# Output projection of the second block's mixer: the gate goes into the weights of columns 512 to 1023, on GpSimd

## The chip, the core and the metric

The kernel runs on one core of a Trainium2 chip, as one launch. Its time is device microseconds of that core. Several runs are made; the median counts. One further execution is recorded by the hardware profiler, and all rows of a trace in this document come from such an execution. The engines are TensorE (PE, its weight loads PEld), VectorE (DVE), ScalarE (ACT), GpSimd (POOL) and SyncE (SP, which here only issues transfers). All work side by side and wait for one another through semaphores.

## The reference

Two transformer blocks of different kinds run one after the other on 256 tokens of width 1024, all in float32. The first has an mLSTM mixer, a pooling mixer, cross attention and squared-ReLU layers. The second, to which the change belongs, has one layer:

```
mod = c_act @ w_ada[l] + b_ada[l]
sh_a, sc_a, g_a, sh_f, sc_f, g_f = jnp.split(mod[:, None, :], N_MOD, axis=-1)
h = rms_norm(x, g_mix[l]) * (1.0 + sc_a) + sh_a
x = x + g_a * hybrid_mixer(h, ...)      # ends in: return merged @ w_out
h = rms_norm(x, g_ffn[l]) * (1.0 + sc_f) + sh_f
x = x + g_f * swiglu(h, w_gate[l], w_up[l], w_down[l])
...
return rms_norm(x, g_final)
```

hybrid_mixer has four heads of differential attention ("diff") and four of latent attention ("mla"), both causal. merged is 256 x 1024 and w_out 1024 x 1024. The gate g_a is one number per output column, the same for all tokens, so g_a * (merged @ w_out) equals merged @ (w_out with column c times g_a[c]).

## The kernel before, in words

Tokens lie in two tiles of 128 partitions, t = 0 and 1. Each 1 MB piece of a weight ("chunk", 128 x 2048 float32 in SBUF) is loaded by SP into one of four buffers (raw), and then split into a high part in PE's rounded format and a low rest: ACT casts raw into wh (hi_to, line 1193), DVE subtracts, wl = raw - wh (lo_to, line 1841; lo_part, line 1849, in pieces). Activations are split the same way (XH and XL, in the trace XS). PE multiplies high by high, high by low and low by high. A raw buffer is loaded anew once DVE has made wl from it.

The chunks of the output projection are named wout2 0 to 3; each holds 256 rows of w_out with all 1024 columns. They are loaded, cast and split in the order 0, 2, 1, 3, which SP, ACT, DVE and PE follow. PE's rows("wout2", ...) (lines 406, 413 and 421) sums them into four PSUM banks: YB[2t] for columns 0 to 511 of token tile t, YB[2t + 1] for columns 512 to 1023. The last two chunks are summed in one call, tile 0 ahead of tile 1.

Each engine runs one program written out by hand, in the order of its lines; nothing is scheduled later. While PE works on attention, DVE and ACT do its softmaxes between their shares of the weight splits:

- diff_e(h) on DVE (lines 2465 to 2469) scales and subtracts the two softmaxes of a diff head, in a tile U (reciprocal, TENSOR_SCALAR, then twice a TENSOR_SCALAR and a SCALAR_TENSOR_TENSOR). PE's diff_t(h) transposes that tile (line 1012).
- mla_e(h) on DVE (lines 2501 to 2503) scales the softmax of an mla head, also in U, and mla_t(h) transposes it (line 1012).
- diff_v(h): ACT sums squares, POOL makes the reciprocal root (lines 2831 and 2728, named "do"), DVE scales (2477).

Behind the last sum, DVE's gated adds the projection to the residual rows X: a product with the gate's row (line 2590) and an addition (line 2591), for each tile and each half h of the columns:

```
e.wait_ge(*pe_rows[rows, t, h])
e.wait_ge(d_gate, 32)
step(e.tensor_tensor(U[:, t, cs], YB[2 * t + h][:, :], GB[:, n, cs], ALU.mult))
e.tensor_tensor(X[:, t, cs], X[:, t, cs], U[:, t, cs], ALU.add).then_inc(cnt.add(("gated", t, h)))
```

GB (a part of AR) holds the two gates' rows on all partitions; POOL loads it at 627. step lets the engine wait for its own instruction. Then follow the mean square (rms_square, rms_mean, and rsqrt on POOL), the scaled rows U = X * r (rms_z, line 2327, or ACT's line 1537), PE's transposes of U (line 512), and the columns' scale and shift with a new split (ACT lines 1356 and 1361, DVE lines 2073, 2077 and 2082). With these blocks PE starts the first gate and up products of the feed-forward part (pair, line 474). For the last down projection, chunks ("down", 9) and ("down", 10), POOL already multiplies columns 512 to 1023 of raw with the second gate (line 2842) ahead of ACT's cast.

Of the kernel before, what the change touches and what calls it, by code (L numbers as in the profile page):

```python
# [11 lines left out]
ALU = mybir.AluOpType  # L12
# [6 lines left out]
NR = 4  # L19
# [143 lines left out]
def build_program(nc, I, out):  # L163
    ctx = ExitStack()
    with ctx:
        def sb(name, shape, dt=F32):
            return ctx.enter_context(nc.sbuf_tensor(name, shape, dt))

        def sem(name):
            return ctx.enter_context(nc.semaphore(name))  # L170
# [3 lines left out]
        def count(name):  # L174
            counts.append(Count(sem(name)))
            return counts[-1]
# [3 lines left out]
        RAW = [sb(f"raw{i}", [128, CH]) for i in range(NR)]  # L180
        WH = [sb(f"wh{i}", [128, CH], F32R) for i in range(NS)]
        WL = [sb(f"wl{i}", [128, CH], F32R) for i in range(NS)]
        X = sb("X", [128, 2, 1024])
# [22 lines left out]
        YB = [ctx.enter_context(nc.psum_tensor(f"YB{i}", [128, 512], F32)) for i in range(4)]  # L206
# [4 lines left out]
        def cols(key, n):  # L211

            if key not in sm_at:
                a = max((b for _, b in sm_at.values()), default=0)
                sm_at[key] = (a, a + n)
                assert a + n <= 416
            a, b = sm_at[key]
            return SM[:, a:b]
# [41 lines left out]
        GB = AR[:, 6144:8192].rearrange("p (n c) -> p n c", n=2)  # L260
# [43 lines left out]
        N = {c[0]: n for n, c in enumerate(chunks)}  # L304
# [4 lines left out]
        landed = lambda n: (s_raw[n % NR], 16 * sum(len(parts(i)) for i in range(n % NR, n + 1, NR)))  # L309
# [5 lines left out]
        d_idn, d_cols, d_tab, d_mem, d_crow, d_gate, d_ln10, d_gm, d_wm, d_tb, d_lam, d_out0, d_out1 = (  # L315
            sem("in_" + n) for n in "idn cols tab mem crow gate ln10 gm wm tb lam out0 out1".split())
# [8 lines left out]
        w_hi, w_lo, w_hi0, w_lo0, w_ada, w_pool, w_gated, w_lat_hi, w_lat_lo = (  # L325
            count(n) for n in "w_hi w_lo w_hi0 w_lo0 w_ada w_pool w_gated w_lat_hi w_lat_lo".split())
        pe_turn, pe_front, pe_mlstm, pe_rows, pe_xa, pe_mlp, pe_pool, pe_mix, pe_ffn = (
            count("pe_" + n) for n in "turn front mlstm rows xa mlp pool mix ffn".split())
        act_front, act_mlstm, act_y, act_ln, act_xa, act_mlp, act_pool, act_mix, act_ffn = (
            count("act_" + n) for n in "front mlstm y ln xa mlp pool mix ffn".split())  # L330
        dve_zero, dve_front, dve_mlstm, dve_y, dve_ln, dve_xa, dve_mlp, dve_mod, dve_mix, dve_ffn = (
            count("dve_" + n) for n in "zero front mlstm y ln xa mlp mod mix ffn".split())
# [842 lines left out]
        def scalar(e):  # L1175
            at, steps_ = [0], Steps(act_own)

            def hi_to(m):

                while at[0] < len(mms) and at[0] <= m:  # L1180
                    k = at[0]
                    at[0] += 1
                    n = mms[k]
                    name, _, a, b = chunks[n]
                    raw, w = RAW[n % NR], WH[k % NS]
                    e.wait_ge(*(w_gated[n] if name in (("down", 9), ("down", 10)) else landed(n)))
                    if k >= NS:
                        e.wait_ge(*ends.get(k - NS, (act_own, 1)))
                    if name[0] == "qup":
                        for o, s in qup_parts(w, raw):  # L1190
                            f = e.copy(o, s)
                    else:
                        f = e.copy(w[:, 0:a * b], raw[:, 0:a * b])  # L1193
                    f.then_inc(w_hi.add(k))
# [35 lines left out]
            m, n = M["in", 1], N["in", 1]  # L1230
# [26 lines left out]
            for j in range(4):  # L1257
# [5 lines left out]
                for t in range(2):  # L1263
                    W = bank_of.get(("vo", j, t), WB[0])
                    e.wait_ge(*pe_front["vo", j, t])
                    if j < 2:
                        f = e.copy(V1[:, t, 2 * j:2 * j + 2, 0:256], W[:, :].rearrange("p (h c) -> p h c", h=2))
                    else:
                        f = e.activation(OG[:, t, 512 * j - 1024:512 * j - 512], W[:, :], ACT.Sigmoid)
# [514 lines left out]
            r = [cols(("rms", "out", t), 6)[:, 3:4] for t in range(2)]  # L1784
# [4 lines left out]
            for h in range(2):  # L1789
                cs = slice(512 * h, 512 * h + 512)  # L1790
                e.wait_ge(*dve_ffn["g", 0, h])
                f = e.activation(U[:, 0, cs], U[:, 0, cs], ACT.Identity, scale=r[0])
# [15 lines left out]
        def vector(e):  # L1808
            at, steps_ = [0, 0], Steps(dve_own)

            def step(f):
                f.then_inc(steps_.add())
                e.wait_ge(*steps_.now())

            def lo_to(m):


                while at[0] < len(chunks) and at[1] <= m:
                    n = at[0]
                    at[0] += 1  # L1820
                    name, _, a, b = chunks[n]
                    raw = RAW[n % NR]
                    if name[0] == "ada":
                        e.wait_ge(*landed(n))
                        e.wait_ge(d_crow, 32)
                        for i in range(2):
                            w, c = raw[:, 1024 * i:1024 * i + 1024], 2 * name[1] + i
                            f = e.scalar_tensor_tensor(w, w, 1.0, CROW, ALU.mult, ALU.mult, accum_out=MS[:, c:c + 1])  # L1828
                        f.then_inc(w_ada.add(n))
                        continue  # L1830
                    if name in (("pool",), ("lat", 1), ("lat", 2)):
                        continue
                    m_ = at[1]
                    at[1] += 1
                    H, L = WH[m_ % NS], WL[m_ % NS]
                    e.wait_ge(*w_hi[m_])
                    if name[0] == "qup":
                        for (h, s), (l, _) in zip(qup_parts(H, raw), qup_parts(L, raw)):
                            f = e.tensor_tensor(l, s, h.bitcast(F32), ALU.subtract)
                    else:  # L1840
                        f = e.tensor_tensor(L[:, 0:a * b], raw[:, 0:a * b], H[:, 0:a * b].bitcast(F32), ALU.subtract)  # L1841
                    f.then_inc(w_lo.add(m_))
# [19 lines left out]
            for q in range(4):  # L1862
# [10 lines left out]
                if q == 1:  # L1873
                    e.wait_ge(*act_front["gates"])
                    for o, c in ((0, 0), (32, 4)):
                        p = e.tensor_tensor(GL[:, :, o:o + 4], GRAW[:, :, c:c + 4], GH[:, :, o:o + 4].bitcast(F32),
                                            ALU.subtract)
# [708 lines left out]
            def gated(rows, cnt, n, t, h):  # L2586
                cs = slice(512 * h, 512 * h + 512)
# [3 lines that stand above are left out]
                e.tensor_tensor(X[:, t, cs], X[:, t, cs], U[:, t, cs], ALU.add).then_inc(cnt.add(("gated", t, h)))  # L2591

            g, b = lambda k: MC[:, 32 + k:33 + k], lambda k: MC[:, 24 + k:25 + k]
            lo_to(M["gate", 0])
            gated("wout2", dve_mix, 0, 0, 0)
            gated("wout2", dve_mix, 0, 0, 1)
            rms_square("ffn", 0, 1, dve_mix["gated", 0, 1])
            rms_mean("ffn", 0, (act_ln["ms", "ffn", 0, 0], dve_ln["ms", "ffn", 0, 1]))
            lo_part(M["up", 0], 0, 512)
# [1 line left out]
            lo_part(M["up", 0], 512, 1024)  # L2601
            gated("wout2", dve_mix, 0, 1, 0)
            evac("ffn", 0, 1, g, b)
            gated("wout2", dve_mix, 0, 1, 1)
            lo_part(M["up", 0], 1024)
            rms_low("ffn", 0, 0)
            rms_mean("ffn", 1, (act_ln["ms", "ffn", 1, 1],))
# [30 lines left out]
            for t in range(2):  # L2638
                ts = slice(256 * t, 256 * t + 256)
                e.wait_ge(*act_ffn[("g", 0) if t else ("g", 0, "first")])  # L2640
                p = e.tensor_tensor(SU[0][:, ts], YB[t][:, 256:512], SG[0][:, ts], ALU.mult)
# [57 lines left out]
            w, last = cols(("rms", "out", 1), 6), X[:, 1, 768:1024]  # L2699
# [10 lines left out]
        def gpsimd(e):  # L2710
# [16 lines left out]
            def rsqrt(o, x, sem_):  # L2727
                e.tensor_tensor(o, x, MH[:, 0:o.shape[1]], ALU.pow).then_inc(sem_)
# [13 lines left out]
            for h in range(4):  # L2742
                for t in range(2):
                    w = cols(("hc", h, t), 4)
# [45 lines left out]
            n, s_in = bvec("scale", I["pool_scale"][0])  # L2790
            p = N["pool",]
# [3 lines left out]
            for k in range(2):  # L2795
                f = e.tensor_tensor(r4[:, :, k], r4[:, :, k], BV[n][:, :].rearrange("p (g c) -> p g c", g=4), ALU.mult)
# [25 lines left out]
            for t in range(2):  # L2822
                for name, n in (("kl", 256), ("ql", 384)):
                    w = cols((name, t), 2)
                    e.wait_ge(*act_mix[name, t])
                    step(e.tensor_scalar(w[:, 0:1], w[:, 0:1], 1 / n, EPS, ALU.mult, ALU.add))
                    rsqrt(w[:, 1:2], w[:, 0:1], po_mix.add((name, t)))
            for h in range(4):
                w = cols(("do", h), 4)
                e.wait_ge(*act_mix["osq", h])  # L2830
                step(e.tensor_scalar(w[:, 0:2], w[:, 0:2], 1 / 128, EPS, ALU.mult, ALU.add))
                rsqrt(w[:, 2:4], w[:, 0:2], po_mix.add(("do", h)))
            rms_stats("ffn")
            users[:] = [dve_ln["z", "ffn", 1, 1]] * 2
            bvec("final", I["g_final_2"])
            e.wait_ge(d_gate, 32)
            for j in (9, 10):
                n = N["down", j]
                r = RAW[n % NR][:, :].rearrange("p (k c) -> p k c", k=2)
                e.wait_ge(*landed(n))  # L2840
                for k in range(2):
                    f = e.tensor_tensor(r[:, k, 512:1024], r[:, k, 512:1024], GB[:, 1, 512:1024], ALU.mult)
                f.then_inc(w_gated.add(n))
            rms_stats("out", (0,))
            w = cols(("rms", "out", 1), 6)
            e.wait_ge(*act_ln["ms", "out", 1, 1])
# [146 lines left out]
```

## Time and profile before

| | us |
|---|---|
| median of 3 runs (lowest, highest) | 942.92 (942.86, 943.18) |
| the profiled execution's own time | 943.09 |
| its span, first to last instruction | 941.4 |
| PE busy | 932.6 (99%) |
| DVE busy | 706.7 (75%) |
| ACT busy | 519.6 (55%) |
| POOL busy | 61.4 (7%) |

The granted clock of PE is 0.998 of full speed over the span. Busy time alone doesn't tell what an engine is worth to the end: the chain of waits and the timelines do. In a timeline, a row has its start in us from the span's start, its duration, the engine, the line, the operation, output<-input tiles, the form, how many instructions it merges, and in brackets the idle time before it with what ended it. A row of several instructions has the time from the start of the first to the end of the last, and these overlap.

### The profile page before, as it was taken

The numbers are of one execution on the slowest core, as the hardware profiler recorded it, in microseconds if no ns is written. First come the engines' busy times: TensorE is split into PE (matmuls) and PEld (weight loads), VectorE is DVE, ScalarE is ACT, GpSimd is POOL, SyncE is SP. The second block draws the span as 40 slices with busy tenths as digits, with TensorE's granted clock in tenths as the row PEclk, the third lists the DMA queues.
The fourth block names the chain that finished last, engine by engine and source line by source line (L and its number), as shares of the span: only waits on it lengthen the run. The fifth ranks groups of instructions, "written<-read, shape, count | busy, mean of one in ns | idle before, by whom it ended". The sixth has DMA issues, their size and how long they took to land.

```text
span 941.4 us, 13155 instructions
## 1 busy us (share of the span) xinstructions
PE 932.6 (99%) x5121; PEld 808.6 (86%) x5121; DVE 706.7 (75%) x975; ACT 519.6 (55%) x732; POOL 61.4 (7%) x96
## 2 busy tenths in 40 slices
PE   9999999999999999999999999999999999999997
PEld 9889888988888888889888888888998888888886
DVE  6967678688888776888788877678769886556575
ACT  5757463636655555355275555555567675444543
POOL 0000211001000002110100000002100000000020
PEclk9999999999999999999999999999999999999999
DMA  9795374456988885274399888773633475656521
GB/s 327 274 329 179 134 240 166 176 180 226 334 282 292 285 296 194 104 270 137 131 316 326 295 292 283 252 263 128 234 109 115 135 245 182 222 179 194 174 81 45
DMA packets 109660, 203.00 MB, mean 216 GB/s; under 512 B 4332, under 2 KB 75264, under 8 KB 106272
## 3 DMA queue, kind: packets, MB, share of 16 engines
q1 hardware_dynamic: 106000, 189.15, 59.2%
q0 software_dynamic: 3168, 12.24, 3.6%
q8 instruction: 41, 0.67, 0.3%
q10 hardware_dynamic: 432, 0.79, 0.2%
q14 instruction: 19, 0.16, 0.0%
HBM read 201.09 MB, written 1.06 MB: 215 GB/s over the span
## 4 chain that ended last, share of the span: by engine, by line
PE 95%; DVE 2%; ACT 1%; issue 1%; DMA 0%; POOL 0%; POOLq 0%; DVEq 0%; ACTq 0%
PE WB L379 20%; PE YB L406 11%; PE YB L413 11%; PE YB L421 11%; PE WB L385 11%; PE YB L474 6%; PE WB L406 3%; PE WB L359 3%; PE WB L413 3%; PE WB L421 3%; PE WB L366 2%; PE WB L362 2%; PE YB L900 2%; PE WB L512 2%; PE WB L760 1%
## 5 line engine op out<-in xcount | busy, mean ns | idle before, releaser
L1841 DVE TENSOR_TENSOR wl<-raw,wh 128x2048 fp32r<-128x2048 f32 x144 | 331.3, 2307 | 106.8 <-ACT wh L1193 102.0
L1193 ACT CAST wh<-raw 128x2048 fp32r<-128x2048 f32 (+1 forms) x147 | 280.0, 1907 | 35.9 <-PE YB L421 14.8
L379 PE MATMUL WB<-XS,wh 128*128 128x512 f32 x832 | 199.1, 390 | 0.0
L379 PEld LDWEIGHTS WB<-XS,wh 128*128 128x128 f32 x832 | 154.9, 188 | 31.4
L385 PEld LDWEIGHTS WB<-XS,wl 128*128 128x128 f32 x832 | 107.6, 191 | 4.6
L385 PE MATMUL WB<-XS,wl 128*128 128x256 f32 x832 | 109.0, 283 | 0.0
L406 PE MATMUL YB<-wh,FHT 128*128 128x512 f32 x344 | 106.6, 391 | 0.0
L413 PE MATMUL YB<-wl,FHT 128*128 128x512 f32 x344 | 106.2, 390 | 0.0
L421 PE MATMUL YB<-wh,FLT 128*128 128x512 f32 x344 | 106.1, 389 | 0.0
L1384 ACT COPY U<-WB 128x256 f32<-128x256 f32 x102 | 33.0, 376 | 125.9 <-PE WB L385 125.9
L413 PEld LDWEIGHTS YB<-wl,FHT 128*128 128x128 f32 x344 | 64.6, 188 | 13.8
L421 PEld LDWEIGHTS YB<-wh,FLT 128*128 128x128 f32 x344 | 64.6, 188 | 13.7
L406 PEld LDWEIGHTS YB<-wh,FHT 128*128 128x128 f32 x344 | 62.1, 189 | 10.6
L1828 DVE SCALAR_TENSOR_TENSOR raw<-raw,AR 128x1024 f32<-128x1024 f32 x48 | 56.6, 1216 | 0.0
L474 PE MATMUL YB<-wh,XS 128*128 128x512 f32 x160 | 44.1, 401 | 0.0
L406 PE MATMUL YB<-wh,XS 128*128 128x512 f32 x136 | 42.9, 401 | 0.0
L413 PE MATMUL YB<-wl,XS 128*128 128x512 f32 x136 | 41.4, 390 | 0.0
L421 PE MATMUL YB<-wh,XS 128*128 128x512 f32 x136 | 41.3, 390 | 0.0
L1375 ACT CAST XS<-WB 128x512 fp32r<-128x512 f32 x16 | 9.4, 587 | 47.4 <-PE WB L512 47.4
L474 PEld LDWEIGHTS YB<-wh,XS 128*128 128x128 f32 x160 | 28.7, 188 | 6.1 <-ACT XS L1361 0.4
L413 PEld LDWEIGHTS YB<-wl,XS 128*128 128x128 f32 x136 | 25.5, 188 | 5.5
L421 PEld LDWEIGHTS YB<-wh,XS 128*128 128x128 f32 x136 | 25.5, 188 | 5.5
(375 smaller groups left out, 1285.7 us busy)
## 6 DMA issues: line engine op xcount, KB each, us to landing
raw<-in_mlp_w SPq DMA_DIRECT2D x64, 1024.0 KB, 5.3
raw<-in_w_ada_t SPq DMA_DIRECT2D x24, 1024.0 KB, 5.4
raw<-in_mlstm_w_in SPq DMA_DIRECT2D x11, 1024.0 KB, 8.6
raw<-in_w_ffn_down SPq DMA_DIRECT2D x11, 1024.0 KB, 5.0
raw<-in_w_ffn_gate SPq DMA_DIRECT2D x10, 1024.0 KB, 5.5
raw<-in_w_ffn_up SPq DMA_DIRECT2D x10, 1024.0 KB, 5.7
raw<-in_mem_w_kv SPq DMA_DIRECT2D x8, 1024.0 KB, 6.7
raw<-in_xattn_wq SPq DMA_DIRECT2D x8, 1024.0 KB, 7.0
```

The source lines that it names most:

```text
L359: e.matmul(o, H[:, at(k)], xh[:, k, :], start=k == 0, stop=False)
L362: e.matmul(o, L[:, at(k)], xh[:, k, :], start=False, stop=False)
L379: e.matmul(W[:, :], H[:, at(k, f)], XS[:, k, :], start=k == 0, stop=False)
L385: p = e.matmul(W[:, 0:256], L[:, at(k, f)], XH[:, k, :], start=False, stop=k == 7)
L406: e.matmul(o, xh[:, k0 + k, tk], pick(H, k), start=start and k == 0, stop=False)
L413: f = e.matmul(o, xh[:, k0 + k, tk], pick(L, k), start=False, stop=stop and low_last and k == a - 1)
L421: f = e.matmul(o, xl[:, k0 + k, tk], pick(H, k), start=False, stop=stop and not low_last and k == a - 1)
L474: f = e.matmul(YB[t][:, :], x[:, k, 128 * t:128 * t + 128], w[ms[n] % NS][:, 512 * (k % 4):512 * (k % 4) + 512], start=start and k == 0, s ...
L1193: f = e.copy(w[:, 0:a * b], raw[:, 0:a * b])
L1384: p = e.copy(o[:, 256 * f:256 * f + 256], bank_of.get(key + (f,), WB[0])[:, 256:512])
L1828: f = e.scalar_tensor_tensor(w, w, 1.0, CROW, ALU.mult, ALU.mult, accum_out=MS[:, c:c + 1])
L1841: f = e.tensor_tensor(L[:, 0:a * b], raw[:, 0:a * b], H[:, 0:a * b].bitcast(F32), ALU.subtract)
```

## The change

Columns 512 to 1023 of all four wout2 chunks are multiplied with the first gate's row on POOL, in raw, before ACT casts them. ACT's cast of these chunks then waits for POOL (w_gated) in place of the load. POOL does chunks 0 and 2 ahead of its rsqrts for diff heads 0 and 1, and chunks 1 and 3 ahead of those for heads 2 and 3. DVE adds YB[1] and YB[3] to X directly (added, line 2597 of the new file) and leaves the product out. Columns 0 to 511 stay as they were. The two down chunks use the same helper as before their place; only the wait for the gate's row comes earlier on POOL.

```diff
-                    e.wait_ge(*(w_gated[n] if name in (("down", 9), ("down", 10)) else landed(n)))
+                    e.wait_ge(*(w_gated[n] if name in (("down", 9), ("down", 10)) or name[0] == "wout2" else landed(n)))
...
+            def added(t):
+
+                e.wait_ge(*pe_rows["wout2", t, 1])
+                e.tensor_tensor(X[:, t, 512:1024], X[:, t, 512:1024], YB[2 * t + 1][:, :], ALU.add
+                                ).then_inc(dve_mix.add(("gated", t, 1)))
+
             lo_to(M["gate", 0])
             gated("wout2", dve_mix, 0, 0, 0)
-            gated("wout2", dve_mix, 0, 0, 1)
+            added(0)
...
-            gated("wout2", dve_mix, 0, 1, 1)
+            added(1)
...
+            def gate_second(w, n):
+
+                r = RAW[n % NR][:, :].rearrange("p (k c) -> p k c", k=2)
+                e.wait_ge(*landed(n))
+                for k in range(2):
+                    f = e.tensor_tensor(r[:, k, 512:1024], r[:, k, 512:1024], GB[:, w, 512:1024], ALU.mult)
+                f.then_inc(w_gated.add(n))
+
+            e.wait_ge(d_gate, 32)
             for h in range(4):
+                if h in (0, 2):
+                    gate_second(0, N["wout2", h // 2])
+                    gate_second(0, N["wout2", 2 + h // 2])
                 w = cols(("do", h), 4)
...
-            e.wait_ge(d_gate, 32)
             for j in (9, 10):
-                n = N["down", j]
-                r = RAW[n % NR][:, :].rearrange("p (k c) -> p k c", k=2)
-                e.wait_ge(*landed(n))
-                for k in range(2):
-                    f = e.tensor_tensor(r[:, k, 512:1024], r[:, k, 512:1024], GB[:, 1, 512:1024], ALU.mult)
-                f.then_inc(w_gated.add(n))
+                gate_second(1, N["down", j])
```

On POOL, between the latents' rsqrts (lines 2826 and 2728) and the diff heads' (2831 and 2728), before:

```order
L2826 TENSOR_SCALAR SM<-SM 128x1
L2728 TENSOR_TENSOR SM<-SM 128x1
L2831 TENSOR_SCALAR SM<-SM 128x2
L2728 TENSOR_TENSOR SM<-SM 128x2
L2831 TENSOR_SCALAR SM<-SM 128x2
```

and after, where raw1, raw2, raw3 and raw0 are the buffers of wout2 0, 2, 1 and 3:

```order
L2832 TENSOR_SCALAR SM<-SM 128x1
L2734 TENSOR_TENSOR SM<-SM 128x1
L2839 TENSOR_TENSOR raw1<-raw1,AR 128x512 x2
L2839 TENSOR_TENSOR raw2<-raw2,AR 128x512 x2
L2849 TENSOR_SCALAR SM<-SM 128x2
L2734 TENSOR_TENSOR SM<-SM 128x2
L2849 TENSOR_SCALAR SM<-SM 128x2
L2734 TENSOR_TENSOR SM<-SM 128x2
L2839 TENSOR_TENSOR raw3<-raw3,AR 128x512 x2
L2839 TENSOR_TENSOR raw0<-raw0,AR 128x512 x2
L2849 TENSOR_SCALAR SM<-SM 128x2
```

Four products have come in ahead of the first two rsqrt pairs of the diff heads, and four between the second and the third.

On DVE, at the sums of the output projection, with the mean square of tile 0 behind the first piece and the split of the feed-forward part's second chunk behind the second:

```order
 L2590 TENSOR_TENSOR U<-YB,AR 128x512
 L2591 TENSOR_TENSOR X<-X,U 128x512
-L2590 TENSOR_TENSOR U<-YB,AR 128x512
-L2591 TENSOR_TENSOR X<-X,U 128x512
+L2597 TENSOR_TENSOR X<-X,YB 128x512
 L2334 SCALAR_TENSOR_TENSOR AR,SM<-X 128x512
 L2343 TENSOR_SCALAR SM<-SM 128x1
```

In both tiles two instructions have become one; nothing else moved on DVE, and PE and ACT have the same instructions in the same order.

## Rows read from the trace of the kernel before

**Rows 1.** The page, chain that ended last, share of the span by engine.
```profile
PE 95%; DVE 2%; ACT 1%; issue 1%; DMA 0%; POOL 0%; POOLq 0%; DVEq 0%; ACTq 0%
```

**Rows 2.** Timeline of DVE, sums of the output chunks: start us, us, line op, idle before.
```profile
744.73 0.68 DVE L2590 TENSOR_TENSOR U<-YB,AR 128x512 f32<-128x512 f32 x1
745.45 0.69 DVE L2591 TENSOR_TENSOR X<-X,U 128x512 f32<-128x512 f32 x1
748.24 0.48 DVE L2327 TENSOR_SCALAR U<-X,SM 128x512 f32<-128x512 f32 x1 [0.45 <-POOL SM L2728]
```

**Rows 3.** Timeline of PE, same stretch and just behind it.
```profile
747.87 0.61 PE L421 MATMUL YB<-wh,XS 128*128 128x512 f32 x2
748.78 0.66 PE L512 MATMUL WB<-IDN,U 128*128 128x128 f32 x4 [0.29 <-DVE U L2327]
751.02 1.39 PE L474 MATMUL YB<-wh,XS 128*128 128x512 f32 x4
752.25 1.09 PE L474 MATMUL YB<-wl,XS 128*128 128x512 f32 x4
```

**Rows 4.** Timeline of POOL, products with the gate for two later chunks.
```profile
897.31 3.87 POOL L2842 TENSOR_TENSOR raw<-raw,AR 128x512 f32<-128x512 f32 x2 [139.84 <-DMA raw<-in_w_ffn_down]
903.08 2.66 POOL L2842 TENSOR_TENSOR raw<-raw,AR 128x512 f32<-128x512 f32 x2 [1.91 <-DMA raw<-in_w_ffn_down]
```

**Rows 5.** The four output chunks on the SP queue, their landing, SP and DVE timelines.
```profile
L2871 SPq DMA_DIRECT2D raw<-in_w_out x4: 367/368/368, 676.0 to 703.3; - x4
DMA to landing us min/median/max: 4.7/4.9/5.1
...
693.93 9.78 SPq L2871 DMA_DIRECT2D raw<-in_w_out  x3
...
685.39 0.29 DVE L2439 SCALAR_TENSOR_TENSOR U<-WB,bv 128x128 f32<-128x128 f32 x1 [3.90 <-PE WB L1005]
```

**Rows 6.** Timelines of POOL (first row), DVE and PE (last row), 706 to 713.
```profile
706.37 0.70 POOL L2728 TENSOR_TENSOR SM<-SM 128x2 f32<-128x2 f32 x1
...
708.05 2.28 DVE L1841 TENSOR_TENSOR wl<-raw,wh 128x2048 fp32r<-128x2048 f32 x1
710.44 0.29 DVE L2502 TENSOR_SCALAR U<-U,SM 128x128 f32<-128x128 f32 x1
710.64 0.35 DVE L2503 TENSOR_SCALAR U<-U,SM 128x256 f32<-128x256 f32 x1
...
712.20 0.49 PE L1012 MATMUL WB<-IDN,U 128*128 128x128 f32 x3
```

**Rows 7.** Timelines of ACT (first row), DVE and PE (last row), 697 to 706.
```profile
705.89 1.91 ACT L1193 CAST wh<-raw 128x2048 fp32r<-128x2048 f32 x1
...
697.11 2.28 DVE L1841 TENSOR_TENSOR wl<-raw,wh 128x2048 fp32r<-128x2048 f32 x1
699.51 0.23 DVE L2466 TENSOR_SCALAR SM<-SM 128x2 f32<-128x2 f32 x1
700.62 0.49 DVE L2469 SCALAR_TENSOR_TENSOR U<-U,SM 128x256 f32<-128x256 f32 x1
...
702.19 0.49 PE L1012 MATMUL WB<-IDN,U 128*128 128x128 f32 x3
```

**Rows 8.** Timeline of DVE beside the later products; last row: one form elsewhere.
```profile
898.24 1.78 DVE L2635 TENSOR_TENSOR FLT<-AR,FHT 128x512 fp32r<-128x512 f32 x1
899.95 3.38 DVE L1841 TENSOR_TENSOR wl<-raw,wh 128x2048 fp32r<-128x2048 f32 x1
903.25 0.74 DVE L1997 TENSOR_TENSOR AR<-WB,U 128x256 f32<-128x256 f32 x2
...
L2635 DVE TENSOR_TENSOR FLT<-AR,FHT x2: 683/684/686, 848.5 to 865.1; 128x512 fp32r<-128x512 f32 x2
```

**Rows 9.** Timelines of POOL (first row) and DVE near 660.
```profile
659.72 0.42 POOL L2826 TENSOR_SCALAR SM<-SM 128x1 f32<-128x1 f32 x1
...
659.67 0.42 DVE L2399 TENSOR_SCALAR U<-U,SM 128x384 f32<-128x384 f32 x1 [0.72 <-POOL SM L2728]
```

## The prediction

> **What bounds the kernel now.** I read the chain of waits first. The reader is to see in it that 95% of the span is matmul work and that DVE holds 2% [rows 1]. So a change on DVE, ACT or POOL is worth only what TensorE (PE) stands still for, and it costs what it newly makes PE stand still. Next I read the timelines of PE and DVE around the output chunks' last sums. The piece of DVE work that PE waits for there is short: the product with the gate starts at 744.73, its addition at 745.45, and the scaled rows U are ready at 748.24 + 0.48 = 748.72 [rows 2]. PE's last two matmuls before them start at 747.87 and take 0.61 together. Matmuls of 512 columns follow each other every 0.23 us: the four at 752.25 need until 753.17, which is 0.92. So the next instruction could start at 747.87 + 2 x 0.23 = 748.33, and it starts at 748.78 [rows 3]. That is a stall of 0.45 us. Behind it come four matmuls in 751.02 to 752.25 = 1.23 instead of 0.92 [rows 3]: another 0.31 us of short waits, for the blocks of the normalised rows.
>
> **What DVE gets back.** Each of the two additions of columns 512 to 1023 loses its product. From one addition's end to the next this is 745.45 - 744.73 = 0.72 us [rows 2], twice. The first lies on the path to PE: U is then ready at 748.72 - 0.72 = 748.00, before PE asks for it at 748.33, and the stall of 0.45 goes whole. What is late next is PE's own row of matmuls. The second product, and the 0.72 that the first one already gave, pull forward the DVE block among the 0.31. The other block in it comes from ACT, behind PE's own transposes. I take half of 0.31, 0.15. So the gain is 0.45 + 0.15 = 0.60, with bounds 0.45 and 0.45 + 0.31 = 0.76.
>
> **What POOL's work costs by itself.** There are eight new products of 128x512 on POOL, two per chunk. The same instruction exists for two later chunks: two of them take 2.66 us where nothing is in the way, so 1.33 each, and 3.87 where something is [rows 4]. Against ACT's splits they are hidden. The four chunks are issued between 676.0 and 703.3, the second at 693.93, and land about 4.9 later. The first is multiplied near 681, where DVE idles for 3.90 until 685.39, the second near 700 [rows 5]. The third and fourth follow POOL's rsqrt for head 1 (of the diff heads), which ends at 706.37 + 0.70 = 707.07 [rows 6], so they are done by about 714. ACT's cast of the first starts at 705.89 [rows 7], those of the others later, in the order 0, 2, 1, 3 of the chunks and with other work between; none is to wait. On POOL's queue stand behind the products only rsqrts, which wait for sums that ACT makes later. So in time of its own this part costs nothing, neither on ACT nor on POOL.
>
> **What they do to DVE.** This is the term that decides. In the two rows with 3.87, DVE ran beside POOL. Its subtraction of 128x512 at 898.24 took 1.78 where the same takes 0.684 elsewhere, and the 128x2048 at 899.95 took 3.38, not 2.28 [rows 4, 7, 8]. The first ends at 900.02, the second at 903.33 and not at 900.02 + 2.28 = 902.30, so it was held for 1.03 us; the first took 1.10 more than elsewhere. POOL and DVE took turns, and each POOL product held DVE for about 1.0. Two products with an input in PSUM, at 903.25 beside POOL's at 903.08, took 0.74 for the pair, 0.37 each; that shows no hold [rows 4, 8]. Does a DVE instruction with a single SBUF input, a TENSOR_SCALAR on U, collide too? In the other direction there is a sign of it: POOL's one-column instruction at 659.72 lasts 0.42 and ends at 660.14, just behind DVE's TENSOR_SCALAR from 659.67 to 660.09 [rows 9]. I take it as colliding.
>
> The Trainium skill (SBUF — State Buffer, "Who interferes with whom") has this as an exclusive lock on a port pair: a DVE instruction with two SBUF inputs, or one in a two-port mode, and a GpSimd instruction block each other for the whole instruction. The trace agrees that it is a block and not a slowdown in proportion, but holds 1.0 of the 1.33 us; by the whole instruction each hold would be 0.33 dearer, place A 0.66 and the sum below about +1.0.
>
> **Place A, second chunk, near 700.** The chunk lands at about 693.93 + 4.9 = 698.8. POOL starts at 699.0, finds DVE in its 2.28 from 697.11, and gets its turn at 699.39 until about 700.35. DVE's softmax scaling of head 1 (reciprocal, then five instructions from 699.51 on, the last from 700.62 to 701.11) is held [rows 7]: its first TENSOR_SCALAR moves from 699.51 to 700.35, by 0.84. The second product asks at about 700.65 and gets its turn before one of the instructions that wait for their predecessor, for another 1.0. So U is ready at 701.11 + 1.84 = 702.95. PE transposes it at 702.19 [rows 7]. With 0.06 from a DVE end to PE's start (748.72 to 748.78) PE stalls 702.95 + 0.06 - 702.19 = 0.82. The bounds are 0, if only one hold falls there (0.84 is less than the slack of 702.19 - 701.11 - 0.06 = 1.02), and 1.4 with three times 1.0 less some overlap. From there on PE, ACT, DVE and POOL are all 0.82 later together. What stands behind the held instructions on DVE is the sum for the mla heads' rotated part and the split of a later weight, and then DVE waits for POOL's next rsqrt anyway, so nothing else is late.
>
> **Place B, third and fourth chunk, near 710** (times without the 0.82). The first product holds 707.15 to 708.4. DVE wants its 2.28 at 708.05 [rows 6], starts 0.3 later and ends at 710.6. The second product then has its turn until 711.65. DVE's scaling of the mla head's U, at 710.44 and 710.64 [rows 6], starts at 711.65 instead of 710.44, 1.21 later, and ends at 710.99 + 1.21 = 712.20. PE transposes that U at 712.20, so it stalls 0.06, say 0.1. The third product asks for its turn about 0.2 after its start (1.33 less the 1.0 held and less 0.13 between the release and its recorded end: 897.31 + 3.87 = 901.18 [rows 4], with DVE free 2.28 before 903.33, at 901.05), so at 711.98. DVE's second instruction is there 0.2 behind the first, at 711.85. I take DVE as first, but by 0.13 us only. The instructions behind it read PSUM, and then DVE has idle time again. The bounds are 0 and 1.1, the latter if the third product comes first.
>
> **Sum.** -0.60 + 0.82 + 0.10 = +0.32 us. The profiled execution took 943.09 (span 941.4), so it would be 943.4. The median of the runs is 942.92, 0.17 below, so the prediction is 943.2.
>
> **The rivals.**
> 1. Both places cost in full: POOL's third product at place B comes ahead of DVE's 710.64, and U is 1.0 later. -0.60 + 0.82 + 1.1 = +1.3, so 944.2. For it speaks how small the 0.13 is; against it, that in [rows 4, 8] each turn went to the engine that had asked first. The same section of the Trainium skill says that issue order decides who blocks; those rows agree.
> 2. The holds do not reach PE. If a TENSOR_SCALAR is not held by POOL ([rows 9] show only the other direction), place A loses about 1 us of DVE, within its slack of 1.02, and place B nothing. Then only the gain is left: -0.6, so 942.3.
> 3. Slower beyond what can be measured. Each product at place B catches DVE: 4 x 1.03 = 4.1, less a slack of 712.20 - 0.06 - 710.99 = 1.15, is 2.9. With 0.82 and a gain of 0.45 only, this is +3.3, so 946.2. It decides from the third hold on (3.1 - 1.15 = 1.9, and 1.9 + 0.82 - 0.60 = +2.1), and needs PSUM-reading instructions to be held or a DVE queue without idle time. The two products at 903.25 speak against it.
>
> **How the numbers follow.** The forecast has 0.46, rival 1 0.24, rival 2 0.18, rival 3 0.09. For a cause that I don't see, faster by over 0.2%, 0.03 is left: the stalls of PE that hang on DVE's products come to 0.76 at most. 0.2% is 1.9 us, about what a measurement of this kernel can tell from no change. The forecast's own range is 942.8 to 943.8; the range that takes in rivals 1 and 2 is 942.2 to 944.7. Within 0.2%: 0.46 + 0.24 + 0.18 = 0.88, of which 0.02 go to slower because rival 1 with a hold more lands near +1.9; slower 0.11, faster 0.03.
>
> **What would show it.** In the changed kernel's trace, each of the eight products on POOL stands at 1.33 or longer. Near 700 DVE's 128x256 scaling of U ends about 1.8 later than its neighbours' shift, and PE has a wait of about 0.8 for U before the transposes (L1012), then at most 0.1 near 713. ACT's casts of the output chunks have no wait for POOL. The stall of 0.45 before L512 is gone, and U of L2327 comes ahead of PE. The forecast is wrong if PE has no new wait near 702, if the wait near 713 is near 1, or if ACT waits for POOL.

## The result, and the profile after

| | before | changed |
|---|---|---|
| median of 13 runs (lowest, highest) | 943.09 (942.86, 944.09) | 945.15 (944.87, 946.74) |
| span of the profiled execution | 941.4 | 943.4 |
| DVE busy | 706.7 | 709.0 |
| POOL busy | 61.4 | 73.8 |

The changed kernel takes 2.06 us more; the ratio is 1.0023, with a 95% interval of 1.0015 to 1.003. It lies outside the stated range (942.2 to 944.7), on the slow side. DVE's busy time rose although two of its instructions are gone. The two products were taken away (2 x 0.68 = 1.36), and busy time still rose by 2.3, so about 3.7 us of holds have come: instructions of DVE that stand longer beside POOL's products. The rows of places A and B below show five of them, 0.83 + 1.11 + 0.13 + 0.83 + 1.03 = 3.93.

The chain that ended last, to set beside [rows 1]: DVE has a percent more.

```profile
PE 94%; DVE 3%; ACT 1%; issue 1%; DMA 0%; POOL 0%; POOLq 0%; DVEq 0%; ACTq 0%
```

The list of PE's waits (engine, line, who released it: us in total, times, longest) has two entries that the kernel before lacks; the one at L569 is at the start and was there too:

```profile
PE WB L1012 <- DVE U L2440: 1.2, 1, 1.2
PE WB L569 <- DVE XS L1856: 1.2, 1, 1.2
PE WB L1012 <- DVE U L2469: 0.8, 1, 0.8
```

Place A, near 700. The timelines of POOL (first row), DVE and PE (last row), to set beside [rows 7]:

```profile
698.88 2.89 POOL L2839 TENSOR_TENSOR raw<-raw,AR 128x512 f32<-128x512 f32 x2 [14.31 <-DMA raw<-in_w_out]
...
699.50 1.06 DVE L2466 TENSOR_SCALAR SM<-SM 128x2 f32<-128x2 f32 x1
700.47 1.40 DVE L2468 TENSOR_SCALAR U<-U,SM 128x128 f32<-128x128 f32 x1
701.90 0.35 DVE L2469 SCALAR_TENSOR_TENSOR U<-U,SM 128x128 f32<-128x128 f32 x1
702.17 0.35 DVE L2468 TENSOR_SCALAR U<-U,SM 128x256 f32<-128x256 f32 x1
702.55 0.48 DVE L2469 SCALAR_TENSOR_TENSOR U<-U,SM 128x256 f32<-128x256 f32 x1
...
703.18 0.52 PE L1012 MATMUL WB<-IDN,U 128*128 128x128 f32 x3 [0.85 <-DVE U L2469]
```

In the kernel before, the first L2468 is

```profile
699.65 0.29 DVE L2468 TENSOR_SCALAR U<-U,SM 128x128 f32<-128x128 f32 x1
```

DVE's TENSOR_SCALAR on two columns (L2466) takes 1.06 where it took 0.23, the next one (L2468) 1.40 instead of 0.29. These are the two products, one hold each, of 0.83 and 1.11. All behind them takes what it did. The last scaling of U ends at 703.03, and PE transposes at 703.18 what it transposed at 702.19: 0.99 later.

Place B, near 712, to set beside [rows 6]:

```profile
708.03 7.11 POOL L2839 TENSOR_TENSOR raw<-raw,AR 128x512 f32<-128x512 f32 x4
...
709.06 2.41 DVE L1841 TENSOR_TENSOR wl<-raw,wh 128x2048 fp32r<-128x2048 f32 x1
711.58 1.12 DVE L2502 TENSOR_SCALAR U<-U,SM 128x128 f32<-128x128 f32 x1
712.63 1.38 DVE L2503 TENSOR_SCALAR U<-U,SM 128x256 f32<-128x256 f32 x1
713.93 0.28 DVE L2439 SCALAR_TENSOR_TENSOR U<-WB,bv 128x128 f32<-128x128 f32 x1
714.13 0.41 DVE L2440 SCALAR_TENSOR_TENSOR U<-WB,bv 128x256 f32<-128x256 f32 x1
715.10 0.87 DVE L2485 TENSOR_SCALAR AR<-WB,PC 128x256 f32<-128x256 f32 x2
...
714.60 0.55 PE L1012 MATMUL WB<-IDN,U 128*128 128x128 f32 x3 [1.23 <-DVE U L2440]
```

Here POOL's four products take 7.11 us. DVE's weight split (L1841) is held for 0.13, and the two scalings (L2502 and L2503) for 0.83 and 1.03. Thus both scalings take a hold, where the prediction had one for L2502 alone. The third product by itself stands at its usual length, so it had the turn from its start, and L2503, whose record starts 0.05 later, waited for it:

```profile
712.58 1.28 POOL L2839 TENSOR_TENSOR raw<-raw,AR 128x512 f32<-128x512 f32 x1
```

The fourth product (713.82 to 715.14) held nothing: beside it stand DVE's instructions that read PSUM (L2439 and L2440) and the two maxima of U, which read SBUF (TENSOR_REDUCE, 714.57 and 714.78, 0.29 and 0.41), all at their usual length.

PE's transpose starts at 714.60 instead of 712.20, so 2.40 later, 1.41 of it new. The reader is to see that it does not start behind L2503, which ends at 714.01 with U complete. It starts at the end of L2440, 714.13 + 0.41 = 714.54. Behind the next transposes and scores PE's L359 is 2.70 late, before and after:

```profile
713.78 0.62 PE L359 MATMUL WB<-FHT,wh 128*128 128x256 f32 x3
716.48 0.62 PE L359 MATMUL WB<-FHT,wh 128*128 128x256 f32 x3
```

The sums of the projection, DVE and then PE, for [rows 2, 3]:

```profile
747.44 0.68 DVE L2597 TENSOR_TENSOR X<-X,YB 128x512 f32<-128x512 f32 x1
750.22 0.49 DVE L2327 TENSOR_SCALAR U<-X,SM 128x512 f32<-128x512 f32 x1 [0.45 <-POOL SM L2734]
...
750.57 0.62 PE L421 MATMUL YB<-wh,XS 128*128 128x512 f32 x2
751.02 0.60 PE L512 MATMUL WB<-IDN,U 128*128 128x128 f32 x4
754.24 1.09 PE L474 MATMUL YB<-wl,XS 128*128 128x512 f32 x4
```

U of L2327 is complete at 750.71, and PE's transposes follow its matmuls without a pause: 751.02 - 750.57 = 0.45, two matmuls. Set against the same instructions before, PE is 750.57 - 747.87 = 2.70 late ahead of the transposes, 751.02 - 748.78 = 2.24 at them, and 754.24 - 752.25 = 1.99 behind the first block. So the gain is 0.46 + 0.25 = 0.71. The whole account is 0.99 + 1.41 + 0.30 - 0.71 = 1.99 us, against 2.0 between the two spans. The 0.30 is 2.70 less 2.40; it arises between 714.60 and 716.48 (see why the prediction was wrong).

ACT's casts of the first two chunks come at their old place, 1.0 later like all else (705.89 and 708.58 before), and wait for nothing on POOL:

```profile
706.90 1.90 ACT L1193 CAST wh<-raw 128x2048 fp32r<-128x2048 f32 x1
709.58 1.90 ACT L1193 CAST wh<-raw 128x2048 fp32r<-128x2048 f32 x1
```

### The profile page after: what moved, and what is told of

The parts are those of the page before. It is cut to its first block, busy times and chain, and to the rows that moved or that the text cites. A ratio compares the mean times of both kernels' runs of the same rounds, so it can differ in the third digit from the quotient of the medians.

```text
span 943.4 us, 13159 instructions
## 1 busy us (share of the span) xinstructions
PE 932.6 (99%) x5121; PEld 808.6 (86%) x5121; DVE 709.0 (75%) x973; ACT 519.6 (55%) x732; POOL 73.8 (8%) x104
## 3 DMA queue, kind: packets, MB, share of 16 engines
HBM read 201.09 MB, written 1.06 MB: 214 GB/s over the span
## 4 chain that ended last, share of the span: by engine, by line
PE 94%; DVE 3%; ACT 1%; issue 1%; DMA 0%; POOL 0%; POOLq 0%; DVEq 0%; ACTq 0%
PE WB L379 20%; PE YB L406 11%; PE YB L413 11%; PE YB L421 11%; PE WB L385 11%; PE YB L474 6%; PE WB L406 2%; PE WB L413 2%; PE WB L421 2%; PE WB L359 2%; PE WB L366 2%; PE WB L362 2%; PE YB L900 2%; PE WB L512 2%; PE WB L760 1%
## 5 line engine op out<-in xcount | busy, mean ns | idle before, releaser
L1841 DVE TENSOR_TENSOR wl<-raw,wh 128x2048 fp32r<-128x2048 f32 x144 | 331.0, 2305 | 106.9 <-ACT wh L1193 102.1
L474 PEld LDWEIGHTS YB<-wh,XS 128*128 128x128 f32 x160 | 28.7, 188 | 5.8 <-ACT XS L1361 0.4
L2839 POOL TENSOR_TENSOR raw<-raw,AR 128x512 f32<-128x512 f32 x12 | 19.2, 1623 | 174.8 <-DMA raw<-in_w_ffn_down 141.9
```

Source lines behind the costliest of these rows:

```text
L474: f = e.matmul(YB[t][:, :], x[:, k, 128 * t:128 * t + 128], w[ms[n] % NS][:, 512 * (k % 4):512 * (k % 4) + 512], start=start and k == 0, s ...
```

## The experiments

Times are medians. Each kernel ran beside the kernel before on the same chip; before was 943.08 to 943.15 in these groups.

| kernel | us | ratio to before (95%) |
|---|---|---|
| dve_alone | 942.30 | 0.9991 (0.9982 to 1.0) |
| pool_alone | 945.76 | 1.0028 (1.0017 to 1.0039) |
| chunks_02 | 943.41 | 1.0004 (0.9995 to 1.0013) |
| chunks_13 | 943.99 | 1.001 (1.0 to 1.0019) |
| chunks_021 | 944.02 | 1.001 (1.0001 to 1.0019) |
| bank_first | 944.24 | 1.0013 (1.0004 to 1.0022) |
| moved | 942.78 | 0.9996 (0.9987 to 1.0005) |
| moved_split | 942.32 | 0.9993 (0.9984 to 1.0002) |
| one_input, one execution | 942.57 | |
| one_input_timed | 942.36 | 0.9991 (0.9982 to 1.0001) |

**dve_alone.** Out of the changed kernel:

```diff
-                    e.wait_ge(*(w_gated[n] if name in (("down", 9), ("down", 10)) or name[0] == "wout2" else landed(n)))
+                    e.wait_ge(*(w_gated[n] if name in (("down", 9), ("down", 10)) else landed(n)))
...
-                if h in (0, 2):
-                    gate_second(0, N["wout2", h // 2])
-                    gate_second(0, N["wout2", 2 + h // 2])
```

> The changed kernel without POOL's eight products on the output chunks, and with ACT's cast waiting for the load as before; this leaves the gate out of columns 512 to 1023 of the projection. Theory of the holds: DVE's shorter sums are worth what they save PE and nothing else costs, so about 0.7 us faster than before (the shift of PE between 748 and 752 in the changed kernel went from 2.70 to 1.99): 942.4 by a median of 943.1 before, no wait of PE at L1012, none before L512. Rival, that the change's loss lies in the sums themselves (an addition straight from PSUM) or in what DVE does behind them: not faster, 943 to 945.

Measured: 942.30 beside 943.11, -0.8 us. PE has no wait at L1012. Its timeline at the transposes shows two matmuls' time from 747.82 to 748.28, for [rows 3]:

```profile
747.82 0.62 PE L421 MATMUL YB<-wh,XS 128*128 128x512 f32 x2
748.28 0.60 PE L512 MATMUL WB<-IDN,U 128*128 128x128 f32 x4
```

DVE's part of the change is a gain. The prediction gave it 0.60, with 0.76 as the upper bound, so 0.8 is a little more than that; between 747.8 and 752 this trace gains 0.73 on before, near the changed kernel's 0.71. The rival falls.

**pool_alone.**

```diff
-            added(0)
+            gated("wout2", dve_mix, 0, 0, 1)
...
-            added(1)
+            gated("wout2", dve_mix, 0, 1, 1)
```

> POOL's eight products and ACT's wait for them as in the changed kernel, but DVE multiplies by the gate as before too, so the gate stands twice in columns 512 to 1023. Theory of the holds: all of the loss is here, 2.7 us over before (945.8), PE waits of 0.85 and 1.23 at L1012, and the stall of about 0.45 before L512 as in the kernel before. Rival, that gain and loss lie elsewhere and add up differently: below +2.2 or above +3.2.

Measured: 945.76, +2.65 us. PE's waits hold both entries and the old stall at L512 again:

```profile
PE WB L1012 <- DVE U L2440: 1.2, 1, 1.2
PE WB L1012 <- DVE U L2469: 0.9, 1, 0.9
PE WB L512 <- DVE U L2327: 0.3, 1, 0.3
```

All of the loss is with POOL's products. The two parts, -0.81 and +2.65, add up to +1.84, 0.2 short of the +2.06 measured for both.

**chunks_02.** The products and the wait on w_gated for chunks 0 and 2 only:

```diff
-                if h in (0, 2):
-                    gate_second(0, N["wout2", h // 2])
-                    gate_second(0, N["wout2", 2 + h // 2])
+                if h == 0:
+                    gate_second(0, N["wout2", 0])
+                    gate_second(0, N["wout2", 2])
```

> The changed kernel with POOL's products on chunks 0 and 2 alone (columns 512 to 1023 of chunks 1 and 3 have no gate). Theory of the holds by place: place A costs 1.0, place B nothing, gain 0.7, so +0.3 over before (943.4), one wait of PE at L1012 of 0.85 near 703 and none near 714. Rival, that lateness from place A makes part of the wait at B: a second wait at L1012 remains and the time is above +0.8.

Measured: 943.41, +0.3. One wait at L1012 is left. Place A alone costs what was expected and leaves nothing for place B:

```profile
PE WB L1012 <- DVE U L2469: 0.9, 1, 0.9
```

**chunks_13.** The same edit with chunks 1 and 3 (at h == 2).

> The changed kernel with POOL's products on chunks 1 and 3 alone (columns 512 to 1023 of chunks 0 and 2 have no gate), so place B without place A. Theory of the bank and the holds, with additive places: B costs 1.7 us (1.4 at the second L1012, 0.3 at L1004 behind it), no wait at the first L1012, gain 0.7, so +1.0 over before, 944.1. Rival, that the wait at B depends on the lateness that A leaves: less than +0.6.

Measured: 943.99, +0.84, and the other wait alone:

```profile
PE WB L1012 <- DVE U L2440: 1.2, 1, 1.2
```

In its trace the second L1012 is at 713.64 for 712.20 before, 1.44 late, with another 0.3 by the end of L1004's group, as in the changed kernel. So place B costs the same without place A. The two runs, +0.30 and +0.84, add up to +1.14; as each holds the gain, 0.71 of it has to be added once more, and that is +1.85, again 0.2 short of +2.06.

**chunks_021.** The same edit with chunks 0 and 2 at h == 0, and chunk 1 at h == 2.

> The changed kernel with POOL's products on chunks 0, 2 and 1, not on chunk 3 (whose columns 512 to 1023 have no gate). At place B two products are left, the ones that hold DVE's weight split by 0.1 and its first scaling of U by 0.85, so U and all behind it are 0.98 late there. Theory of the bank: PE's transposes (L1012) wait for the PSUM bank that DVE's L2440 frees behind the scaling, with a slack of only 0.62 (712.20 less 0.06 less 711.52 in the kernel before), and PE's L1004 behind them for L2485. So place B costs 0.36 at L1012 and about 0.65 in all, the kernel is +1.0 + 0.65 - 0.7 = +0.9 over before, 944.0. Rival, the prediction's own slack of 1.15, for U itself: place B costs nothing with two products, +0.3, 943.4.

Measured: 944.02, +0.94, the theory's number; the rival's 943.4 is missed by 0.6. PE's waits, then DVE's timeline:

```profile
PE WB L1012 <- DVE U L2469: 0.9, 1, 0.9
PE WB L1012 <- DVE U L2440: 0.2, 1, 0.2
...
711.88 1.13 DVE L2502 TENSOR_SCALAR U<-U,SM 128x128 f32<-128x128 f32 x1
712.93 0.34 DVE L2503 TENSOR_SCALAR U<-U,SM 128x256 f32<-128x256 f32 x1
713.39 0.41 DVE L2440 SCALAR_TENSOR_TENSOR U<-WB,bv 128x256 f32<-128x256 f32 x1
```

With two products at place B only L2502 is held (1.13), and L2503 takes its 0.34. This is just the order of turns that the prediction took, with U complete at 712.93 + 0.34 = 713.27, one microsecond late. It had PE stall 0.1 there. PE stalled until 713.85, behind L2440's end at 713.80, and place B as a whole cost 0.68 in this trace (PE is 1.28 late at place A's transposes and 1.96 behind place B, at L359).

**bank_first.** In the order of DVE:

```diff
-            mla_e(0)
             mla_in(1)
+            mla_e(0)
             mla_max(1)
```

> The changed kernel with mla_in(1) ahead of mla_e(0) on DVE, so that the instructions that read PSUM and free the bank stand in front of the scaling of U that POOL's products hold; the maxima stay behind. Theory of the bank: part of the second hold falls beside the PSUM instructions, the wait at the second L1012 falls from 1.23 to about 0.8 and is now for U itself (DVE L2503), the time is about 0.5 below the changed kernel's 945.15, 944.6. Rival, that PE waited for U and not for the bank: wait and time as in the changed kernel or longer.

Measured: 944.24, +1.16 over before and so 0.9 below the changed kernel, where 0.5 was expected. DVE's rows, then PE's:

```profile
711.60 0.41 DVE L2440 SCALAR_TENSOR_TENSOR U<-WB,bv 128x256 f32<-128x256 f32 x1
712.11 0.60 DVE L2502 TENSOR_SCALAR U<-U,SM 128x128 f32<-128x128 f32 x1
712.63 1.38 DVE L2503 TENSOR_SCALAR U<-U,SM 128x256 f32<-128x256 f32 x1
...
714.16 0.52 PE L1012 MATMUL WB<-IDN,U 128*128 128x128 f32 x3 [0.80 <-DVE U L2503]
```

L2440 now ends at 712.01, long before PE needs it, and PE starts at 714.16 behind L2503's end at 714.01. With the bank free, U decides. This is the clearest of the tests: U is complete at the same 714.01 as in the changed kernel, and yet PE starts 0.44 earlier, so in the changed kernel it was not U that PE waited for. The size was expected too small: the maxima, now right behind L2503, end 0.65 earlier than in the changed kernel (714.54 for 715.19), L2485 comes that much earlier behind them, and PE's L1004 loses only 0.09 instead of 0.30. That makes 0.44 + 0.21 = 0.65 in the traces; the remaining 0.25 between the medians is not explained.

**moved.** Out of the changed kernel:

```diff
-                if h in (0, 2):
-                    gate_second(0, N["wout2", h // 2])
-                    gate_second(0, N["wout2", 2 + h // 2])
+                if h == 0:
+                    gate_second(0, N["wout2", 0])
+                    e.wait_ge(*dve_mix["e", 1])
+                    gate_second(0, N["wout2", 2])
+                if h == 2:
+                    e.wait_ge(*dve_mix["in", "m", 1])
+                    gate_second(0, N["wout2", 1])
+                    e.wait_ge(*dve_mix["e", 2])
+                    gate_second(0, N["wout2", 3])
```

> All of the change, but POOL's products moved to stretches in which DVE has no work that PE waits for: chunk 2 behind diff_e(1), chunk 1 behind the DVE pieces of mla_in(1), chunk 3 behind diff_e(2). Theory of the holds: the holds fall on the split of a later weight and on instructions that read PSUM, so nothing of them reaches PE; about 0.7 us faster than before, 942.4, no wait of PE at L1012. Rival, that eight more products on POOL cost PE time wherever they stand (the held DVE work comes back later): between 943.5 and 945.

Measured: 942.78, -0.33, between the theory's 942.4 and the rival's 943.5. No wait at L1012, but a new one. The timelines of POOL and PE:

```profile
701.28 3.34 POOL L2839 TENSOR_TENSOR raw<-raw,AR 128x512 f32<-128x512 f32 x2 [15.87 <-DVE U L2469]
705.17 0.70 POOL L2734 TENSOR_TENSOR SM<-SM 128x2 f32<-128x2 f32 x1
...
706.56 1.21 PE L359 MATMUL WB<-XS,wh 128*128 128x256 f32 x8 [0.28 <-DVE AR L2477]
```

DVE's split of the small weight (L1839) and POOL's products held each other; the two products took 3.34. The rsqrt behind them on POOL ended 0.78 later than before (705.17 + 0.70, for 705.09), and PE waited 0.28 at L359 for the bank that DVE empties with it.

**moved_split.** As moved, but of chunk 2 one product goes ahead of that rsqrt and one behind it:

```diff
                 if h == 0:
                     gate_second(0, N["wout2", 0])
                     e.wait_ge(*dve_mix["e", 1])
-                    gate_second(0, N["wout2", 2])
+                    gate_second(0, N["wout2", 2], (0,))
+                if h == 1:
+                    gate_second(0, N["wout2", 2], (1,))
```

> As moved, but of chunk 2 only the first product stands behind diff_e(1), and the second behind POOL's rsqrt for diff head 0. In moved, both came ahead of that rsqrt, which ended at 705.87 instead of 705.09, and PE waited 0.3 at L359 for the bank that DVE frees with it. Theory of the holds: that wait goes too, the shift of PE against before is none until 748 and -0.7 behind, so 942.4, as in dve_alone. Rival, that the rest of moved's cost is held DVE work and not the late rsqrt: 942.8 again.

Measured: 942.32, -0.76, with the full computation, and no new wait of PE. POOL's rows and DVE's:

```profile
701.38 1.40 POOL L2839 TENSOR_TENSOR raw<-raw,AR 128x512 f32<-128x512 f32 x1 [16.80 <-DVE U L2469]
704.73 0.70 POOL L2734 TENSOR_TENSOR SM<-SM 128x2 f32<-128x2 f32 x1
705.39 1.28 POOL L2839 TENSOR_TENSOR raw<-raw,AR 128x512 f32<-128x512 f32 x1
...
701.55 3.04 DVE L1839 TENSOR_TENSOR wl<-raw,wh 128x768 fp32r<-128x768 f32 x4
```

DVE is still held: the four splits take 3.04 and not 1.96. But this work has time. It is the version that lies below both kernels, 2.8 us below the changed one. Against before the interval of the ratio still takes in 1, while its 11 runs (942.21 to 942.62) all lie below the 27 of before beside them (942.72 to 943.42).

**one_input and one_input_timed.** In gate_second, for the output chunks:

```diff
-                    f = e.tensor_tensor(r[:, k, 512:1024], r[:, k, 512:1024], GB[:, w, 512:1024], ALU.mult)
+                    f = e.tensor_scalar(r[:, k, 512:1024], r[:, k, 512:1024], 1.0, None, ALU.mult)
```

> The changed kernel, POOL's eight products replaced by a multiplication by the constant 1.0, in the same place and of the same size but with a single input in SBUF (columns 512 to 1023 have no gate). Theory that a hold lasts as long as POOL reads SBUF, whatever the number of inputs: DVE's L2466, L2468, L2502 and L2503 are still held, each for a bit less than POOL's instruction takes, by 0.5 to 1.0, and PE waits at L1012 in both places, but less if the instruction is shorter. Rival, that the second input (the gate's row) makes the conflict: no hold, no wait at L1012, 942.4.

> The same kernel as one_input, timed. Its one look showed holds of 0.1 to 0.4 on DVE's scalings and no wait of PE at L1012. Theory that a POOL instruction with one input holds DVE too shortly to reach PE: as dve_alone, 942.3 to 942.5. Rival, that the one look was lucky: 943 or more.

Measured: 942.57 in one execution, 942.36 as the median of ten. There is no wait at L1012. POOL's rows, then DVE's, of the first:

```profile
699.01 3.46 POOL L2842 TENSOR_SCALAR raw<-raw 128x512 f32<-128x512 f32 x2 [14.08 <-DMA raw<-in_w_out]
707.27 7.56 POOL L2842 TENSOR_SCALAR raw<-raw 128x512 f32<-128x512 f32 x4
...
699.75 0.37 DVE L2466 TENSOR_SCALAR SM<-SM 128x2 f32<-128x2 f32 x1
700.61 0.51 DVE L2468 TENSOR_SCALAR U<-U,SM 128x256 f32<-128x256 f32 x1
701.16 0.71 DVE L2469 SCALAR_TENSOR_TENSOR U<-U,SM 128x256 f32<-128x256 f32 x1
710.67 0.44 DVE L2502 TENSOR_SCALAR U<-U,SM 128x128 f32<-128x128 f32 x1
```

POOL's instructions stand in the same places and are longer (3.46 for the two beside place A). DVE's TENSOR_SCALARs take 0.37 for 0.23, 0.51 for 0.35 and 0.44 for 0.29, and its SCALAR_TENSOR_TENSOR (L2469), which reads two inputs in SBUF, 0.71 for 0.49. Both my theory (holds of 0.5 to 1.0) and its rival (none at all) were wrong: there are holds, but of 0.14 to 0.22. They use up part of the slack and no more. This run changed the operation along with the number of inputs, so which of the two makes the holds short was not separated.

## Why the prediction was wrong

Between the two traces +1.99 was measured for +0.32. Of the 1.67 in between, place B makes 1.61, place A 0.17, and the gain takes back 0.11.

**The gain** was right: the stall of 0.45 before L512 went, 0.46 measured, and of the short waits behind it 0.25 went instead of 0.15 (0.71 for 0.60).

**POOL's own time and ACT's wait** were right: nothing.

**The holds** were right in kind and size. TENSOR_SCALARs with one SBUF input are held as taken, by 0.83, 1.11, 0.83 and 1.03, for 1.0 each. The instructions that read PSUM took their usual time: 0.41 for L2440 with POOL's last product beside it.

**Place A** was right: 0.82 predicted; in the trace U is 1.92 later, for 1.84, and PE 0.99. The rest of the difference is that PE starts 0.15 behind this U (703.03 to 703.18), where 0.06 was taken.

**Place B is the step that failed**: "DVE's second instruction is there 0.2 behind the first, at 711.85. I take DVE as first, but by 0.13 us only", and with it the slack of PE. 0.10 was predicted, 1.71 measured, in two parts.
- The turn. The third product came ahead of L2503. I had let it ask 0.2 after its start, behind L2503. In the trace it starts at 712.58 and takes 1.28, with no wait in it, and L2503 starts at 712.63 and is held for 1.03. By chunks_021, which lacks only chunk 3's two products, and 944.02 beside 945.15, this costs 1.1 us. That was rival 1, with a chance of 0.24.
- The wait. "PE transposes that U at 712.20, so it stalls 0.06" took PE to wait for U alone, with a slack of 1.15. But mla_t(0) also takes a PSUM bank. The banks go round in fours, and this one is freed by mla_in(1), the pair L2439 and L2440 behind the scaling on DVE. Before, L2440 ended at 711.52 (unrounded), so the slack is 712.20 - 0.06 - 711.52 = 0.62. Then, by the order of the banks in the program, L1004 waits for the one that L2485 frees, behind two maxima; this is the 0.30. With the prediction's own order of turns (chunks_021) place B costs 0.68 and not 0.10. bank_first shows the same from the other side. The row of before:

```profile
711.10 0.41 DVE L2440 SCALAR_TENSOR_TENSOR U<-WB,bv 128x256 f32<-128x256 f32 x1
```

So rival 1 as written, 944.2, was short as well: it had 1.1 for place B, without the 0.6 of the bank. Rival 3 had four holds there, began from the same wrong slack of 1.15, and came out too long, since the fourth product held nothing. The range ended at 944.7 because both ends of place B (0 and 1.1) were built on that one slack.

The Trainium skill (SBUF — State Buffer, "Who interferes with whom") says, of a VectorE instruction in a two-port mode or with two SBUF inputs beside a GpSimd one, that the one to issue first gets the shared pair for the whole instruction and the other blocks fully. For products with two SBUF inputs on POOL the traces agree up to the size: a hold of 0.8 to 1.1 of about 1.3 us (in which mode the held TENSOR_SCALARs ran, no run shows). For POOL's instruction with one input they differ: it takes about 1.5 us, holds DVE's TENSOR_SCALARs for 0.14 to 0.16, and DVE's L2469 with its two SBUF inputs for 0.22; L2469 ran from 701.16 to 701.87, all of it within POOL's second instruction (700.95 to 702.47). The measurement decides: not every GpSimd instruction that reads SBUF costs DVE its whole length.

What stays open is how turns are given when both engines ask within a tenth of a microsecond. Four traces (changed, pool_alone, bank_first, chunks_13) gave POOL the turn ahead of L2503, and in each the third product's record starts 0.04 to 0.05 ahead of L2503's. That would fit a turn for the first to start. But at place A the second product starts at 700.49, behind L2468 at 700.47, and had the turn all the same. Nothing varied these distances.

## What to carry to other kernels

Work that is put on an idle GpSimd is not free while VectorE works on SBUF: four of the eight products held VectorE for about 1 us each, against two savings of 0.72, and where they were placed the holds landed on what TensorE waits for. Place it, by a wait if need be, beside VectorE work that nobody is waiting for or that reads PSUM; here that made +2.06 into -0.76. And to find the slack of a waiting engine, list all that its instruction needs, the buffer that it writes too: behind the data of interest, the same queue may hold the instruction that frees that buffer.

## What the runs showed of the hardware that was not expected

- A GpSimd TENSOR_SCALAR with one SBUF input (128x512, about 1.5 us) holds a VectorE TENSOR_SCALAR by 0.14 to 0.16 us and a SCALAR_TENSOR_TENSOR by 0.22; a GpSimd TENSOR_TENSOR with two inputs (about 1.3 us) holds a TENSOR_SCALAR by 0.83 to 1.11.
- A small VectorE instruction is held as well: the TENSOR_SCALAR on two columns went from 0.23 to 1.06, a hold of 0.83, as long as that of L2502 on 128 columns.
- Not every VectorE instruction with one SBUF input is held: two TENSOR_REDUCEs beside the fourth product took 0.29 and 0.41, as before.
- It works both ways: beside L1841, which takes 2.28 alone and 2.43 there, POOL's pair needed 4.60 in chunks_021, where the pair at 683 took 2.52.
